# Opening of a two-block kernel: load order, ScalarE order and matmul order of the first two weight tiles

## What is computed

```python
def rms_norm(x, gain):
    xf = x.astype(jnp.float32)
    y = xf * lax.rsqrt(jnp.mean(xf * xf, axis=-1, keepdims=True) + EPS)
    return (y * gain.astype(jnp.float32)).astype(x.dtype)

def hgrn2_mixer(x, w_in, w_out, gate_norm, lower_bound):
    """x (B,L,D); w_in (D,4D) columns = [q | f | i | g]; lower_bound (D,) in [0,1)."""
    proj = x @ w_in
    q, f, i, g = jnp.split(proj, 4, axis=-1)
    f32 = f.astype(jnp.float32)
    lb = lower_bound.astype(jnp.float32)
    forget = lb + (1.0 - lb) * jax.nn.sigmoid(f32)
    ...
h = h + hgrn2_mixer(rms_norm(h, attn_norm[0]), ...)
h = h + conv_ffn(rms_norm(h, ffn_norm[0]), ...)
```

## Time and profile before

| | us |
|---|---|
| median of 3 runs | 1641.46 |
| lowest, highest | 1641.18, 1643.82 |
| the profiled execution, device time | 1640.68 |
| its span | 1638.8 |
| PE busy in it | 1603.5 (98%) |
| DVE, ACT, POOL busy | 1210.3, 980.0, 93.5 |

### The profile page before, as it was taken

One profiled execution on the slowest core, in us unless ns is written; L12 is line 12 of the kernel. 1 busy time (PEld: TensorE's weight loads), 2 busy tenths in 40 slices (PEclk: granted clock), 3 DMA queues, 4 the chain that ended last, 5 costly groups with the idle time before them and its releaser, 6 DMA issues.

```text
span 1638.8 us, 29149 instructions
## 1 busy us (share of the span) xinstructions
PE 1603.5 (98%) x9941; PEld 1392.5 (85%) x9941; DVE 1210.3 (74%) x2085; ACT 980.0 (60%) x1709; POOL 93.5 (6%) x90
## 2 busy tenths in 40 slices
PE   8999999999999999999999999999999999999998
PEld 7887888888788888888879978888888889878887
DVE  5868877779777778766665977666866668676666
ACT  7465766665676667555566465555755557665554
POOL 5000000003100001000000000000090000000000
PEclk9999999999999999999999999999999999999999
DMA  9446666685366667766665557666566665436662
GB/s 268 143 129 192 193 187 188 184 166 130 99 174 194 187 191 221 223 189 189 189 203 160 175 169 214 187 190 191 167 196 189 189 192 164 131 120 204 189 188 86
DMA packets 393608, 292.67 MB, mean 179 GB/s; under 512 B 33419, under 2 KB 365476, under 8 KB 393152
## 3 DMA queue, kind: packets, MB, share of 16 engines
q1 hardware_dynamic: 390448, 280.83, 59.1%
q0 software_dynamic: 2944, 10.80, 2.0%
q10 hardware_dynamic: 144, 0.07, 0.0%
HBM read 290.59 MB, written 1.07 MB: 178 GB/s over the span
## 4 chain that ended last, share of the span: by engine, by line
PE 89%; DVE 7%; ACT 3%; issue 1%; DMA 0%; SPq 0%; DVEq 0%; ACTq 0%
PE ps L429 27%; PE ps L433 14%; PE ps L406 13%; PE ps L407 13%; PE ps L408 13%; DVE w_lo L397 1%; PE ps L772 1%; ACT w_hi L390 1%; DVE SQ L687 1%; PE ps L765 1%; PE ps L517 1%; DVE H L693 1%; PE ps L1123 1%; PE ps L464 0%; PE ps L465 0%
## 5 line engine op out<-in xcount | busy, mean ns | idle before, releaser
L397 DVE TENSOR_TENSOR w_lo<-raw,w_hi 128x1024 fp32r<-128x1024 f32 x532 | 650.8, 1226 | 30.0 <-ACT w_hi L390 28.7
L390 ACT ACTIVATE w_hi<-raw 128x1024 fp32r<-128x1024 f32 x532 | 548.1, 1050 | 46.1 <-PE ps L408 31.1
L429 PE MATMUL ps<-x_both,w_hi 128*128 128x512 f32 x2016 | 503.2, 391 | 1.9 <-DVE w_lo L397 1.9
L429 PEld LDWEIGHTS ps<-x_both,w_hi 128*128 128x128 f32 x2016 | 369.8, 188 | 74.3 <-issue 1.7
L433 PEld LDWEIGHTS ps<-x_both,w_lo 128*128 128x128 f32 x2016 | 275.4, 190 | 19.6
L433 PE MATMUL ps<-x_both,w_lo 128*128 128x256 f32 x2016 | 282.2, 282 | 0.0
L406 PE MATMUL ps<-w_hi,h_hi 128*128 128x512 f32 x536 | 210.8, 393 | 0.6 <-DVE h_lo L919 0.6
L407 PE MATMUL ps<-w_hi,h_lo 128*128 128x512 f32 x536 | 210.0, 392 | 0.0
L408 PE MATMUL ps<-w_lo,h_hi 128*128 128x512 f32 x536 | 208.6, 389 | 0.0
L1004 DVE TENSOR_TENSOR gs<-ps,us 128x256 f32<-128x256 f32 x88 | 37.3, 424 | 186.1 <-ACT us L842 185.8
L842 ACT ACTIVATE us<-ps 128x256 f32<-128x256 f32 x88 | 33.7, 383 | 224.7 <-PE ps L433 224.7
(11 more groups left out here) (360 smaller groups left out, 1902.2 us busy)
## 6 DMA issues: line engine op xcount, KB each, us to landing
raw<-in_ffn_w_up SPq DMA_DIRECT2D x176, 512.0 KB, 3.9
raw<-in_ffn_w_down SPq DMA_DIRECT2D x132, 512.0 KB, 4.6
raw<-in_ffn_w_gate SPq DMA_DIRECT2D x88, 512.0 KB, 4.6
raw<-in_hgrn_w_in SPq DMA_DIRECT2D x32, 512.0 KB, 5.2
raw<-in_gmlp_w_in SPq DMA_DIRECT2D x32, 512.0 KB, 4.2
raw<-in_gmlp_w_out SPq DMA_DIRECT2D x16, 512.0 KB, 3.9
raw<-in_hgrn_w_out SPq DMA_DIRECT2D x8, 512.0 KB, 3.6
raw<-in_dsa_w_in SPq DMA_DIRECT2D x16, 256.0 KB, 4.7
```

The source lines that it names most:

```text
L390: nc.scalar.activation(w_hi[:, s, :], raw[:, s, :], ACT.Copy).then_inc(hi_done, 1)
L397: nc.vector.tensor_tensor(w_lo[:, s, :], raw[:, s, :], w_hi[:, s, :].bitcast(F32), ALU.subtract)\
L429: pe.matmul(o, whi[:, k, :], x_both[:, k, :, :].rearrange("p a l -> p (a l)"), start=k == 0, stop=False, skip_group_check=True)
```

## The change

1. SP issues the first half of x ahead of weight chunk 0, and the second half behind it.
2. GpSimd waits for the second half of x (`in_x1`) before its first small load, so that all 16 of them, the constants, the positions and the bucket biases follow it.
3. ScalarE takes the sum of squares of the first half ahead of chunk 0's high half, and that of the second half behind the high halves of chunks 1 and 2; the square root comes behind it, with chunk 3 behind that.
4. PE's first two tiles are in a function of their own. Tile 0 does high by high and low by high for each block as soon as its `x_hi` is there, and the 8 products with `x_lo` behind these. Tile 1 waits for its high half only, does 16 products with it, waits for its low half and does the last 8.
5. The spread moves from behind tile 1 into the middle of tile 2. The turning of the small vectors stays behind tile 2.
6. VectorE makes the low halves of chunks 1 and 2 ahead of the row factors, and chunk 3 ahead of the copy to `R`.

```diff
+        def opening(pe, c0):
+            (h0, l0), (h1, l1) = (wv((c0 + t) % RING, KT) for t in range(2))
+            o = ps[:, 0, 0:L]
+            pe.wait_ge(S("gain0"), 1)
+            for k in range(KT):
+                pe.wait_ge(*x_tiles("x_hi_done", "hg", k + 1))
+                if k == 0:
+                    pe.wait_ge(hi_done, c0 + 1)
+                pe.matmul(o, h0[:, k, :], x_hi[:, k, :], start=k == 0, stop=False)
+                if k == 0:
+                    pe.wait_ge(lo_done, c0 + 1)
+                pe.matmul(o, l0[:, k, :], x_hi[:, k, :], start=False, stop=False)
+            for k in range(KT):
+                pe.wait_ge(*x_tiles("x_lo_done", "hg", k + 1))
+                mm = pe.matmul(o, h0[:, k, :], x_lo[:, k, :], start=False, stop=k == KT - 1)
+            mm.then_inc(used, 1)
+            o = ps[:, 1, 0:L]
+            pe.wait_ge(hi_done, c0 + 2)
+            for n, x in enumerate((x_hi, x_lo)):
+                for k in range(KT):
+                    pe.matmul(o, h1[:, k, :], x[:, k, :], start=not n and not k, stop=False)
+            pe.wait_ge(lo_done, c0 + 2)
+            for k in range(KT):
+                mm = pe.matmul(o, l1[:, k, :], x_hi[:, k, :], start=False, stop=k == KT - 1)
+            mm.then_inc(used, 1)
...
-            for t in range(16):
+            opening(pe, c0)
+            for t in range(2, 16):
                 pe.wait_ge(lo_done, c0 + t + 1)
-                if t == 0:
-                    pe.wait_ge(S("gain0"), 1)
                 if t >= 4:
                     pe.wait_ge(S("hg_fq"), t - 3)
-                feat_tile(pe, ps[:, t % 4, 0:L], c0 + t, x_wait="hg" if t == 0 else None).then_inc(used, 1)
-                if t == 1:
+                o = ps[:, t % 4, 0:L]
+                if t == 2:
+                    feat_tile(pe, o, c0 + t, part=range(0, 4))
                     pe.wait_ge(S("fills"), 2)
                     pe_spread(pe, "hg")
+                feat_tile(pe, o, c0 + t, part=range(4, KT) if t == 2 else None).then_inc(used, 1)
                 if t == 2:
                     pe.wait_ge(S("in_vec"), 16 * VDMAS[0])
...
+            act.wait_ge(S("in_x0"), 16)
+            row_square(act, 0)
             split_hi(act, 0)
-            for tb in range(TB):
-                act.wait_ge(S(f"in_x{tb}"), 16)
-                row_square(act, tb)
             act.wait_ge(S("gain0"), 1)
             act_turned(act, "hg", lambda j: ("attn_norm", j), 0)
-            split_hi(act, 1)
+            for c in range(1, 3):
+                split_hi(act, c)
+            act.wait_ge(S("in_x1"), 16)
+            row_square(act, 1)
             act.wait_ge(S("fills"), 2)
             row_root(act, "hg")
-            for c in range(2, HI_AHEAD):
+            for c in range(3, HI_AHEAD):
                 split_hi(act, c)
...
             dve_turned(dve, "hg", lambda j: ("attn_norm", j))
-            split_lo(dve, 1)
+            for c in range(1, AHEAD):
+                split_lo(dve, c)
             dve_roots(dve, "hg")
-            for c in range(2, AHEAD):
-                split_lo(dve, c)
+            split_lo(dve, AHEAD)
             dve_spread(dve, "hg")
...
             for t in range(16):
-                split_lo(dve, c0 + t + AHEAD)
+                if t:
+                    split_lo(dve, c0 + t + AHEAD)
...
             sp.dma_start(vec_loads[0][0], vec_loads[0][1]).then_inc(S("in_gain0"), 16)
-            load(sp, 0, chunks[0])
             for tb in range(TB):
                 sp.dma_start(H[:, tb, :], T["x"][0, tb * P:tb * P + P, :]).then_inc(S(f"in_x{tb}"), 16)
+                if tb == 0:
+                    load(sp, 0, chunks[0])
...
             pool.wait_ge(S("fills"), 1)
+            pool.wait_ge(S("in_x1"), 16)
             for dst, src in vec_loads[1:]:
                 pool.dma_start(dst, src).then_inc(S("in_vec"), 16)
```

## The result

The changed kernel takes 1644.22 us (median of 22 runs, 1641.12 to 1646.88), the kernel before, run beside it, 1641.48 us (22 runs, 1640.18 to 1645.48). The ratio is 1.0013 with an interval of 1.0007 to 1.0018, or +2.1 us (+1.1 to +3.0). The forecast was 1642.3 with a range of 1640.3 to 1644.6: the time is in the range, the sign and the case (A) hold, and +0.8 us is too small. A ratio and its interval come from all the executions of a set and are not the quotient of the two medians: these lie 2.7 us apart here and 1.4 and 1.5 in the two repeats. The profiled execution took 1642.78 us with a span of 1640.9, 2.1 more than that of before.

The account below looks back on a forecast made before the run. PE, busy 98% of the span, bounds the kernel and hands the opening on unchanged. Tile 2 ending 1.9 us ahead, then a 2.7 us wait for the small vectors, gives +0.8 us on 1641.46: 1642.3 us, range 1640.3 to 1644.6.

Parts of the forecast that it names:

- the sign: Whole kernel: slightly slower, +0.8 us; chance 0.93 that it counts as the same within 0.2%.
- the case (A): Opening: the wait for the small vectors takes the place of the waits removed, +0.8 us; chance 0.52.
- The frame: PE, busy 98%, hands on any gain or loss before 20 us one for one; only the opening counts.
- late bound: PE's turning of the vectors: last small load lands at 22.7 us at the latest, +1.4 us.
- The order of the loads: SP's loads: x's first half by 5.9 us, chunk 0 by 7.1, x's second half at 8.4 (8.1 to 8.7).
- Tiles 0 and 1: Opening on PE: x_hi starts at 9.0 us, tile 0 ends at 13.3, tile 1 at 16.2 without waiting.
- The spread: Inside tile 2: costs its 0.36 us as before, no wait, cover 0.2 us; tile 2 ends 1.9 us ahead.
- reciprocal and diagonal at 16.8 to 17.4: VectorE ahead of the spread: both steps done by 17.4 us, before PE is half through tile 2 at 17.6.
- The added wait: GpSimd: small loads start at 8.5 us, last lands at 22.1; PE waits 2.7 us behind tile 2, sum +0.8 us.
- A price that differs: GpSimd's load flight: 5.8 us taken from the trace, against the skill's fixed 2.0 us, which would land near 18.3.
- Rival B: Opening: last small load lands by 19.4 us, so the 1.9 us gain goes through, 1639.6 us; chance 0.08.
- Rival C: PE's clock falls in the 2.7 us vector wait, costing 1.5 us, 1643.8 us; chance 0.33, with late load 0.05.

Follow-up runs that it names:

- e5: The changed kernel with the diagonals made by scalar_tensor_tensor in place of tensor_scalar; 1642.99 us, ratio 1.001.
- f4: The changed kernel with the turning of the small vectors behind tile 3 in place of tile 2; 1643.74 us, ratio 1.0016.
- f2: The changed kernel with GpSimd's constants, positions and biases ahead of the 16 small loads, behind the same wait; 1645.5 us, ratio 1.0028.
- g1: The changed kernel with unread transposes on PE, 5 ahead of the spread and 8 ahead of the turning; 1644.5 us, ratio 1.002.
- f3: The changed kernel with GpSimd waiting for x's first half, plus idle PE transposes, 8 ahead of x and 4 between its halves; 1640.8 us, ratio 0.9993.
- e1: The changed kernel without GpSimd's wait for the second half of x; 1640.98 us, ratio 0.9989.
- e3: The changed kernel with GpSimd waiting for the first half of x in place of the second; 1640.55 us, ratio 0.9989.
- g3: The changed kernel with GpSimd waiting for the first half of x, measured again on another chip; 1641.11 us, ratio 0.9995.
- e2: The kernel before with only GpSimd's wait for the second half of x added; 1642.93 us, ratio 1.0004.
- g4: The kernel before with GpSimd's wait for x's second half and the splits of chunk 2 ahead of the row factors; one run, 1641.56 us.
- g2: The changed kernel itself, unchanged, in a third set; 1643.0 us, ratio 1.0012.

## Why the prediction was right, and which terms were off

**The frame held.** The moment at which PE reaches the turning decides most of the time, and the opening matters only through it: the table above. The number was partly luck. A with its late bound reaches 1642.9 us, or 1643.4 with the scatter that the forecast allowed; the measured 1644.2, and 1643.6 by the ratio, lie beyond, in the part of the range that was there for C, and no profile shows C's fall in the changed kernel's opening.

**The order of the loads** held. Forecast 5.9, 7.1 and 8.4 (8.1 to 8.7); measured 5.3, 7.1 and 8.5.

**Tiles 0 and 1** were mis-sized by the clock. x_hi started at 9.33 (forecast 9.0) and tile 0 ended at 14.2 (forecast 13.3), since its first twelve matmuls ran 0.21 us apart. The prediction named this (up to 1 us, hidden in A) but left it out of the sum. Tile 1 needed no wait and took its 2.9 us (14.23 to 17.11), as forecast.

**The spread** was wrong. I gave the diagonals 0.5 us and the spread a cover of 0.2; they took 2.1, and PE stood 0.72 us. The step that failed is "reciprocal and diagonal at 16.8 to 17.4": the added wait had moved GpSimd's issues under them, and I asked who waits for GpSimd's loads, but not what else its issues disturb. By e5 the error cost nothing here; in f4, where the vectors were in time and the hold was 3.8 us, PE stood 1.9 us for it.

**The added wait** held as the deciding term, and its size was off in three parts. GpSimd began at 9.13 and not 8.5: x landed 0.1 late and, more, 0.6 us pass between the landing and GpSimd's first load, where PE needs 0.05. The issues took 7.78 us and the flight 5.6 (forecast 5.8). So 22.5 instead of 22.1, which is +1.23 and not +0.8. PE waited 0.99 us, not 2.7, as it came there at 21.4 and not 19.4; that the wait would be shorter didn't change its end.

**A price that differs.** The 19 loads of GpSimd took 5.0 to 6.3 us from issue to landing, 5.7 in the median, though they were issued 8 us later than before. The Trainium skill's 2.0 us of fixed cost (DMA: Bandwidth & Descriptors, "Anatomy of one DMA — SWDGE (gpsimd) path") is not what this kernel shows. By it rival B's condition would have come true: the last load, issued at 16.91, would land near 18.9, ahead of PE.

**Rival B** fell with the flight. **Rival C** stays open. In no profile of the changed kernel did the clock fall behind the vectors' wait, and with waits of 2.43 us (e5) and 2.88 us (f2) it stayed at 1.00; yet 2.35 us in g1 was followed by 0.54, 1.78 us in f3 by 0.50, and 1.77 us in f4 by 0.53. So my condition, a wait longer than 1.77 us, fails both ways: longer waits passed, and one of that length brought the fall. What speaks for C is a count over executions: a mean granted clock of 0.997 or less was found in 17 of 43 executions of the changed kernel and in 10 of 90 of the kernel before, and in 4 of 44 of the kernels without a wait for the vectors (e1, e3, g3, f3). But 11 of the 17 are from the first set, whose kernel before has no clocks on record; like with like it is 6 of 21 against 6 of 57. One stretch at the lower level costs 1.2 us where I could see one (g1, f4), so that more of them in 0.3 - 0.1 to 0.4 - 0.1 of the executions would be worth 0.2 to 0.4 us, an estimate. This is an association: in f4's profile the extra fall stands behind a wait far from the opening, and a profile with the fall in the changed kernel's own wait is missing.

**The rest.** Of the measured +2.1 us, 1.2 (1.1 to 1.6 over three profiles) is the late turning, shown by undoing its cause and by adding to it. Some 0.3 may be the clock. The remainder is inside the interval (+1.1 to +3.0), and the gaps in the score bursts, 0.7 us in one profile, come and go; I don't assign it.

## What to carry over

Before a queue of many small loads is made to wait, add up the whole queue, its start-up, every issue and one flight, and compare the sum with the reader of the *last* one: here sixteen issues and a flight are 14 us behind the event waited for. If the wait is wanted, hang it on the earliest event that does the job; moved from the second half of x to the first it cost nothing. And a queue that is moved in time is moved under other engines' work: look at what VectorE does then, not only at who waits for the loads.

## What the hardware showed that I had not expected

**VectorE's `tensor_scalar` can be held while GpSimd issues loads.** Two instructions on 128x128, 0.48 us together, took 2.1 us (four profiles), 3.8 us (two) and 0.64 to 0.88 us (the two that met only a memset's end). In the changed kernel one of the two took 2.03 us by itself. Each time they ended 0.08 to 0.15 us behind the end of a run of GpSimd's work: 19.29 behind 19.16, the last issue, in the changed kernel, 21.19 behind 21.11, the memset, in f4.

Where they slipped in ahead of the memset, it took 1.85 to 1.87 us instead of 1.82 or 1.83. The Trainium skill (SBUF — State Buffer, "SBUF: two separate sides") has a pair of ports that VectorE and GpSimd share: whichever starts first holds it alone for its whole instruction; it has VectorE want that pair in its two-port modes, in which another page (VectorE: DVE Perf Modes, "Mode 2×_2P — use both read ports for one tensor") puts `tensor_scalar`. The trace agrees that the form matters: `scalar_tensor_tensor` took 0.61 us under the same issues (e5). It differs in the length: by the page one instruction of GpSimd is waited for, here it was a whole run of them, up to four issues of 0.5 to 0.7 us, or those and the memset. And twice (e2, g4) the same instruction took 0.48 us in the middle of the same queue. Which mode the instructions ran in, and whether the pair of ports is the cause, no run here shows; what decides between being held and slipping in is open.

**The flight of a load issued by GpSimd** is 4.6 to 6.6 us, from 0.5 KB to 416 KB, in the kernel before, where the 19 are issued at 1.4 to 10.8 us, and 5.0 to 6.3 us in the changed kernel, at 9.1 to 18.5 us. In e1, e2, e3 and f2 it is 4.2 to 7.5 us. What it is made of, no run here shows.

**PE's level in the opening varies.** Its matmuls went from 0.21 to 0.12 us apart at 12.65 in the changed kernel, at about 14.5 in its third profile (g2) and at 11.3 in e3. The gap between the halves of x, 1.06 to 2.0 us in the kernels with the changed opening, doesn't settle it: e5 had one of 1.58 us and was at 0.12 by 11.6, and in g4, which has the opening of the kernel before and no such gap, the matmuls of tile 0 were 0.21 us apart up to 12.8, where in the kernel before and in e2 they were 0.12 apart from the second on.
